# 64-slot experts: bank copies ahead of the next unit's rounding, the second projections eight units behind, one scatter a unit later

## The reference, cut to what matters

```
for e in range(N_EXPERTS):                                  # 8 experts, D_FF_EXPERT = 3584
    gate, up = split(x @ w_in[e])                           # 1024 x 7168
    out = out + gates[:, e:e+1] * ((silu(gate) * up) @ w_out[e])   # 3584 x 1024
```

## Time and profile before

| | us |
|---|---|
| median of 3 runs (lowest, highest) | 1513.35 (1511.95, 1513.36) |
| the profiled execution | 1512.7 |
| its span, first to last instruction | 1511.0 |
| the experts, PE's first unit to the end | 545.2 to 1511.0 |

### The profile page before, as it was taken

The page is one execution under the profiler, slowest core; times in us unless marked ns, Lnnn a source line. Parts: engine busy times, 40 slices in busy tenths (PEclk is TensorE's granted clock), DMA queues, the critical chain, the costliest instruction groups (busy, mean ns, idle before and its releaser), DMA issues.

```text
span 1511.0 us, 18519 instructions
## 1 busy us (share of the span) xinstructions
PE 1428.3 (95%) x7386; PEld 1210.5 (80%) x7386; DVE 1145.6 (76%) x791; ACT 959.0 (63%) x791; POOL 66.6 (4%) x69
## 2 busy tenths in 40 slices
PE   6999999999999899999989998899999889999996
PEld 6987779999899778877778886778887777888885
DVE  3456664444657578898998888899889899889886
ACT  4334544334444457768877777887777887777774
POOL 1001200000000142000001000001000000000000
PEclk9999999999999979999999999999999999999998
DMA  9554556555464459999999999999999999999990
GB/s 348 183 176 158 195 167 219 176 190 194 141 223 167 140 188 362 357 352 366 392 405 368 356 359 361 390 418 366 364 358 349 386 414 400 357 354 378 364 361 30
DMA packets 158695, 446.89 MB, mean 296 GB/s; under 512 B 7040, under 2 KB 45952, under 8 KB 158608
## 3 DMA queue, kind: packets, MB, share of 16 engines
q1 hardware_dynamic: 156784, 439.38, 79.7%
q0 software_dynamic: 1824, 6.33, 1.3%
HBM read 444.63 MB, written 1.05 MB: 295 GB/s over the span
## 4 chain that ended last, share of the span: by engine, by line
PE 78%; ACT 12%; DVE 9%; issue 1%; DMA 1%; DVEq 0%; POOL 0%; SPq 0%; ACTq 0%; POOLq 0%
PE ps L1396 22%; PE ps L1398 21%; PE ps L1397 21%; ACT whi L824 7%; PE ps L1836 3%; PE ps L1799 3%; PE ps L1800 2%; DVE wlo L945 2%; ACT whi_more L824 2%; DVE wlo_more L945 2%; PE ps L1716 1%; PE ps L1793 1%; DVE wlo L377 1%; DMA raw<-in_ret_w_in 1%; ACT up_rows L863 1%
## 5 line engine op out<-in xcount | busy, mean ns | idle before, releaser
L945 DVE TENSOR_TENSOR wlo<-raw,whi 128x2048 fp32r<-128x2048 f32 x209 | 475.0, 2290 | 66.6 <-ACT whi L824 65.8
L824 ACT ACTIVATE whi<-raw 128x2048 fp32r<-128x2048 f32 x208 | 395.9, 1915 | 125.5 <-PE ps L1398 99.1
L377 DVE TENSOR_TENSOR wlo<-raw,whi 128x2048 fp32r<-128x2048 f32 x81 | 185.8, 2294 | 160.9 <-ACT whi L370 160.9
L370 ACT ACTIVATE whi<-raw 128x2048 fp32r<-128x2048 f32 x83 | 158.7, 1912 | 156.5 <-PE ps L1398 151.4
L1396 PE MATMUL ps<-xT_hi,whi 128*128 128x256 f32 x576 | 164.2, 285 | 6.9 <-DVE wlo L377 6.9
L1396 PE MATMUL ps<-whi,xg_big 128*128 128x512 f32 x420 | 166.8, 397 | 0.0
L1398 PE MATMUL ps<-whi,xg_big 128*128 128x512 f32 x420 | 164.6, 392 | 0.0
L1397 PE MATMUL ps<-wlo,xg_big 128*128 128x512 f32 x420 | 164.4, 391 | 0.0
L1398 PE MATMUL ps<-xT_hi,wlo 128*128 128x256 f32 x576 | 163.8, 284 | 0.0
L1397 PE MATMUL ps<-xT_lo,whi 128*128 128x256 f32 x576 | 163.8, 284 | 0.0
L1396 PEld LDWEIGHTS ps<-xT_hi,whi 128*128 128x128 f32 x576 | 111.5, 193 | 7.7 <-issue 7.3
(11 more groups left out here) (251 smaller groups left out, 2761.7 us busy)
## 6 DMA issues: line engine op xcount, KB each, us to landing
raw<-in_moe_w_in SPq DMA_DIRECT2D x168, 1024.0 KB, 6.7
raw<-in_moe_w_out SPq DMA_DIRECT2D x84, 1024.0 KB, 7.0
more_raw<-in_moe_w_in SPq DMA_DIRECT2D x56, 1024.0 KB, 6.7
more_raw<-in_moe_w_out SPq DMA_DIRECT2D x28, 1024.0 KB, 6.8
raw<-in_ret_w_in SPq DMA_DIRECT2D x24, 1024.0 KB, 5.1
raw<-in_ffn_w_in SPq DMA_DIRECT2D x22, 1024.0 KB, 4.9
raw<-in_ffn_w_out SPq DMA_DIRECT2D x11, 1024.0 KB, 4.9
raw<-in_ret_w_out SPq DMA_DIRECT2D x8, 1024.0 KB, 4.8
```

Source lines behind the costliest of these rows:

```text
L370: nc.scalar.activation(whi[:, u % SPLIT, :], src, ACT.Copy).then_inc(hi_done, 1)
L377: nc.vector.tensor_tensor(wlo[:, u % SPLIT, :], src, whi[:, u % SPLIT, :].bitcast(F32), ALU.subtract).then_inc(lo_done, 1)
L824: nc.scalar.activation(moe_split(n)[0], moe_raw(n), ACT.Copy).then_inc(hi_done, 1)
L945: return nc.vector.tensor_tensor(dst, src, hi.bitcast(F32), ALU.subtract)
```

## The change

It has five parts, and adds or removes no instruction.
1. A small job has its own order of units. Between the last up unit of block 0 and its first out unit lie eight units instead of four (out 0 in units 16 to 19 instead of 12 to 15), and out 1, 2 and 3 come last, in units 32 to 41.
2. `gT_small` becomes two buffers, used in turn by the blocks.
3. ACT's copies of gate and up banks stand ahead of the rounding of the same step (`small_copies`), both gate banks in one step; the turns, Silu, product and low half move to later steps, and the rounding of the product leaves the step of the product (`SMALL_HI`).
4. The product on DVE waits for the low half of the block before it.
5. In all jobs scatter(0) stands behind unit 2 instead of unit 1, and DVE's first add in step 3 instead of step 2. scatter(1) stays behind unit 4 and the second add in step 5.

```diff
+    SMALL_STREAM = [(part, b, q) for part, b in (("gate", 0), ("up", 0), ("gate", 1), ("up", 1), ("out", 0), ("gate", 2),
+                                                 ("up", 2), ("gate", 3), ("up", 3), ("out", 1), ("out", 2), ("out", 3))
+                    for q in range(BLOCK_UNITS[b])]
...
-    SMALL_GATE = BIG_SILU
+    SMALL_GATE = {3: 0, 11: 1, 23: 2, 29: 3}
...
-        gT_small, _ = place("gT_small", [P, 8, P], F32R, at=gT_at)
+        gT_small = [place(f"gT_small{i}", [P, 8, P], F32R, at=gT_at + i * 4096)[0] for i in range(2)]
...
+            def small_copies(i, u):
+
+                if i in SMALL_GATE:
+                    unit_done(act, u + i, 0)
+                    for s in range(BLOCK_UNITS[SMALL_GATE[i]] // 2):
+                        nc.scalar.activation(gate_rows[:, s * BANK:(s + 1) * BANK], ps[:, s, :],
+                                             ACT.Copy).then_inc(gate_copied, 1)
+                if i in SMALL_UP:
+                    unit_done(act, u + i, 0)
+                    for s in range(BLOCK_UNITS[SMALL_UP[i]] // 2):
+                        nc.scalar.activation(up_rows[:, s * BANK:(s + 1) * BANK], ps[:, 2 + s, :],
+                                             ACT.Copy).then_inc(up_copied, 1)
...
                 for i in range(JOB_UNITS):
+                    if SMALL[j]:
+                        small_copies(i, u)
                     moe_hi(j * JOB_UNITS + i + MSPLIT)
...
+                    if 4 * small + b > 0:
+                        dve.wait_ge(small_lo, 4 * small + b)
...
-                        elif i in (2, 5):
-                            t, at = i // 3, 1 + POSITION[j - 1]
+                        elif i in (3, 5):
+                            t, at = i // 5, 1 + POSITION[j - 1]
...
-                    if j > 0 and i == 1:
+                    if j > 0 and i == 2:
                         pe.wait_ge(selT_ready, j)
                         pe.wait_ge(y_lo_done, 2 * j)
                         scatter(0)
```

More of the change, by code:

```diff
@@ L59, in build @@
     BLOCK_UNITS = [4, 4, 4, 2]
[L60 to L63, removed]
+    BIG_STREAM = [(part, b, q) for part, b in (("gate", 0), ("up", 0), ("gate", 1), ("out", 0), ("up", 1), ("gate", 2),
+                                               ("out", 1), ("up", 2), ("gate", 3), ("up", 3), ("out", 2), ("out", 3))
+                  for q in range(BLOCK_UNITS[b])]
+    SMALL_STREAM = [(part, b, q) for part, b in (("gate", 0), ("up", 0), ("gate", 1), ("up", 1), ("out", 0), ("gate", 2),
+                                                 ("up", 2), ("gate", 3), ("up", 3), ("out", 1), ("out", 2), ("out", 3))
+                    for q in range(BLOCK_UNITS[b])]
+    assert EFF == 3 * W + BANK and len(BIG_STREAM) == len(SMALL_STREAM) == JOB_UNITS and U_MOE % SPLIT == 0 and JOB_UNITS % RAW == 0
     HALF = P // 2
@@ L76, in build @@
     BIG_LO = {9: (0, 0), 11: (0, 1), 21: (1, 0), 23: (1, 1), 33: (2, 0), 35: (2, 1), 38: (3, 0)}
-    SMALL_GATE = BIG_SILU
[L78 to L82, removed]
+    SMALL_GATE = {3: 0, 11: 1, 23: 2, 29: 3}
+    SMALL_GATE_TURN = {5: 0, 12: 1, 24: 2, 32: 3}
+    SMALL_UP = {7: 0, 15: 1, 27: 2, 31: 3}
+    SMALL_UP_TURN = {8: 0, 16: 1, 28: 2, 33: 3}
+    SMALL_MUL = {9: 0, 17: 1, 29: 2, 34: 3}
+    SMALL_HI = {10: 0, 18: 1, 30: 2, 35: 3}
+    SMALL_LO = {12: 0, 20: 1, 32: 2, 37: 3}
     GATHER = {i: k for k, i in enumerate((13, 15, 17, 19, 25, 27, 29, 31))}
@@ L407, in again_landed, with moe_source @@
             eng.wait_ge(landed[i % RAW], 16 * (landings(i % RAW, MOE_UNITS) + i // RAW + 1) + 16 * (JOB_UNITS // RAW) * p)
-        def moe_source(i, e):
-            part, b, q = STREAM[i]
+        def moe_source(i, e, small=False):
+            part, b, q = (SMALL_STREAM if small else BIG_STREAM)[i]
             if part == "out":
@@ L479, in _, with moe_unit @@
                 load_unit(sp, U_ATT_OUT + i, 0, att_out[:, 2 * i:2 * i + 2, :], 2)
-            def moe_unit(u, i, e, slot, dst, free):
-                src, rows = moe_source(i, e)
+            def moe_unit(u, i, e, slot, dst, free, small=False):
+                src, rows = moe_source(i, e, small)
                 sp.wait_ge(lo_done, free)
@@ L500, in _ @@
                     back = MRAW if n >= MRAW else RAW
-                    moe_unit(U_MOE + n, i, e, moe_slot(n), moe_raw(n), U_MOE + n - back + 1 if n < RAW or n >= MRAW else U_MOE)
+                    moe_unit(U_MOE + n, i, e, moe_slot(n), moe_raw(n), U_MOE + n - back + 1 if n < RAW or n >= MRAW else U_MOE,
+                             SMALL[j])
             sp.wait_ge(over_ready, 1)
@@ L843, in big_drains @@
                     nc.scalar.activation(gT_hi[:, 4 * s:4 * s + 4, :], bank(6, 4), ACT.Copy).then_inc(big_hi, 1)
-            def small_drains(i, u, small):
[L847 to L851, removed]
+            def small_copies(i, u):
[9 more added lines that the diff above has]
+                                             ACT.Copy).then_inc(up_copied, 1)
+            def small_drains(i, u, small):
                 if i in SMALL_GATE_TURN:
@@ L858, in small_drains @@
                     nc.scalar.activation(act_small[:, 0:w], ps[:, 0, 0:w], ACT.Silu).then_inc(small_silu, 1)
[L859 to L866, removed]
+                if i in SMALL_HI:
+                    b = SMALL_HI[i]
                     c = 2 * BLOCK_UNITS[b]
@@ L869, in small_drains @@
                     act.wait_ge(small_mul, 4 * small + b + 1)
-                    nc.scalar.activation(gT_small[:, 0:c, 0:HALF],
+                    nc.scalar.activation(gT_small[b % 2][:, 0:c, 0:HALF],
                                          hid_small[:, 0:c * HALF].rearrange("p (c n) -> p c n", c=c),
@@ L1321, in small_drains @@
                     dve.wait_ge(small_hi, 4 * small + b + 1)
-                    lo_of(gT_small[:, 0:c, HALF:P], hid_small[:, 0:c * HALF].rearrange("p (c n) -> p c n", c=c),
-                          gT_small[:, 0:c, 0:HALF]).then_inc(small_lo, 1)
+                    lo_of(gT_small[b % 2][:, 0:c, HALF:P], hid_small[:, 0:c * HALF].rearrange("p (c n) -> p c n", c=c),
+                          gT_small[b % 2][:, 0:c, 0:HALF]).then_inc(small_lo, 1)
                 if i in SMALL_MUL:
@@ L1753, in big_unit @@
             def big_unit(i, u, big, job, x, hi, lo, before_gate, before_up):
-                part, b, q = STREAM[i]
+                part, b, q = BIG_STREAM[i]
                 if q == 0 and part == "gate":
@@ L1802, in small_unit @@
             def small_unit(i, u, small, job, hi, lo, before_gate, before_up):
-                part, b, q = STREAM[i]
+                part, b, q = SMALL_STREAM[i]
                 if q == 0 and part == "gate":
@@ L1824, in small_unit @@
                             w = slice((2 * c + half) * BANK, (2 * c + half + 1) * BANK)
-                            last = both(ps[:, 4 + half, :], gT_small[:, 2 * q + c, :], hi[:, w], lo[:, w],
+                            last = both(ps[:, 4 + half, :], gT_small[b % 2][:, 2 * q + c, :], hi[:, w], lo[:, w],
                                         b == 0 and q == 0 and c == 0, b == 3 and q == 1 and c == 1)
```

## The result

| | before | changed |
|---|---|---|
| median of 4 runs on the same chip (lowest, highest), us | 1513.36 (1511.95, 1513.66) | 1490.13 (1484.18, 1492.59) |
| the profiled execution, us | 1512.7 | 1488.92 |
| its span, us | 1511.0 | 1487.2 |

The ratio is 0.9843, 95% interval 0.9812 to 0.9873: faster by 1.6%. The forecast was 1489.5. So the close agreement of the first number is partly luck, and the size of the gain is 23 to 31 us.

What follows compares the result with a forecast made beforehand. PE bounds big jobs; in small jobs no engine is full and DVE waits for ACT's roundings. Terms 31.5 - 10.8 + 4.5 - 2.7 = 22.5, some 23 us with job 7, gave 1489.5 us; range 1481 to 1499.

Steps and rivals of the forecast that it cites:

- the ring of four: Small jobs: rounding i+4 needs PE's unit i; PE may run up to 2.6 us late before DVE goes idle.
- The new wait: PE before scatter(1), for DVE's first add, once in each small job: 3.1 us.
- the 0.43 of the entry: DVE's wait at each entry to a small job, from the big job's last round, said to stay: 0.43 us.
- The clock behind it: Small jobs: PE's lower clock level after the wait before scatter(1), likely in all three, 1.6 us each.
- The term of -10.8: Loss from the wait before scatter(1) in three small jobs: 3 x (2.0 delay + 1.6 lower clock) us.
- The start of the big jobs: Big jobs behind small ones: scatter(1) begins 1.5 us earlier against DVE's work, three times, +4.5 us.
- the 31.5: Gain in us from DVE's 32.8 us of waits in the small jobs going, all but some 1.3.
- More stretches at the lower clock: Small jobs: one more low-clock stretch each, 0.9 us on DVE, -2.7 us; bounds 0 and -13.
- The fourth rival: Small jobs: the clock falls again and again, eight stretches a job, 14 us slower, 1528 us; chance 0.05.
- its room: ACT in small jobs: copies ahead of roundings delay them, but the worked schedule has room to hide it.
- some 3 MB to spare: Transfers: 2.5 of 5.2 MB lying ready are drawn down in a small job, costing nothing.
- If ACT waits for DMA: Named sign that the forecast is wrong: ACT kept waiting for transfers; no size given.

Runs made afterwards that it cites:

- e5: The changed kernel with the bank copies behind the rounding of their step again: 1504.76 us, ratio 0.9942.
- e7: The kernel before with only the copies put ahead of the rounding, in its old steps and order of units: 1495.46 us, ratio 0.9887.
- e2: The changed kernel without part 5 (scatter(0) behind unit 1, first add in step 2): 1490.56 us, ratio 0.985.
- e1: The changed kernel with the first add back in step 2, scatter(0) still behind unit 2: 1475.79 us, ratio 0.9748.
- c0: The changed kernel run again with no edit, on another chip, as yardstick for e1, e2 and e4: 1482.71 us, ratio 0.9793.
- e4: The changed kernel with 13 matmuls that nobody reads ahead of scatter(1) in each small job, filling PE's wait: 1482.13 us, ratio 0.9792.
- e3: The changed kernel with the first add in step 2 and scatter(1) behind unit 5 instead of unit 4: 1480.54 us, ratio 0.9789.
- e6: The changed kernel with 12 of the 14 bank copies of a small job done twice on ACT: 1497.61 us, ratio 0.9885.
- e9: The changed kernel with transfers of the experts issued seven units ahead instead of eight: 1487.97 us, ratio 0.9837.

## Why the prediction was right, and where it was not

- **The bound and the mechanism** (DVE kept waiting through the ring of four by PE's waits): right. PE's waits for copies went, that for the product fell from 3.8 to 0.4 us (nothing above 0.3 was forecast), DVE's idle time went with them, small jobs of 101 to 104 were forecast and 100.4 to 103.3 came. DVE is 98.2 busy in them instead of the 100 named. That the copies' place matters is shown in both directions by e5 (21 us lost) and e7 (16.6 gained). The time of the experts alone, in one profile each, gives the order of the gains: 965.8 us before, 947.1 with the copies ahead (e7), 941.4 with the new order of units and the later steps too (e2), 935.8 to 937.6 with part 5 (the changed kernel), 930.0 with the first add back in step 2 (e1). The step from e7 to e2 goes over two chips and more than one edit; the later second projections were not run by themselves.
- **The new wait**, 3.1 us before scatter(1): right in place, waiter and releaser, 2.9 measured. Its cost with the clock up: 2.0 forecast, 2.2 less the 0.43 of the entry = 1.8 measured.
- **The clock behind it**: 1.6 us in all three small jobs was forecast. It falls in six of twelve, and costs 1.3 to 2.9 where it does. The term of -10.8 was, in the changed kernel's first profile, 2.2 + 5.0 + 3.7 us of DVE's idle time less the 1.3 of the entries = 9.6, and 3.5 + 2.2 + 2.2 - 1.3 = 6.6 in c0. That the idling brings the fall is supported by e4 (0 of 3 where it is filled) and by e3 (3 of 3 behind the moved wait), not proven. The kernel before has the same with its wait of 2.06: the level falls right behind it in jobs 1 and 5 and not in job 3. In job 5:

```profile
1146.43 0.47 PE L1742 MATMUL ps<-y_hi,selT 128*128 128x512 f32 x1 [2.06 <-DVE y_lo L945]
...
1147.10 0.63 PE L1742 MATMUL ps<-y_hi,selT 128*128 128x512 f32 x1
1147.52 0.63 PE L1743 MATMUL ps<-y_lo,selT 128*128 128x512 f32 x1
```

- **The start of the big jobs**, +4.5: right in size where it can be read, 1.5 us (10.6 to 9.1). But the sum books -10.8 and +4.5 under part 5, a loss of 6.3, and e2 shows that taking part 5 away costs 7.9 us instead of giving any back. Two things were missed. Without part 5 the small jobs are no shorter, since the wait before scatter(0) and its falls of the clock come back. And the big jobs get longer: I took the 0.74 before scatter(0) there for all that stood in that place, and it becomes 2.1 once PE enters them early. That the total came out all the same means that some of part 5's worth was booked in the 31.5, which takes all waits of DVE as gone; how much was not measured.
- **More stretches at the lower clock**, -2.7: wrong, none came. The idle time that was to bring them is not there either: 0.38 us for nearly every unit was forecast. In job 1, 42 units of 1.82, the turns (six of some 2.0 and two of 1.0) and the scatters (1.9) are 92 of the 100.4 us. Less the new wait of 2.9 that leaves 5.5, or 0.13 a unit: the 2.20 - 1.82 had left out the turns. The longest wait that is left is 0.8, and the clock stays at its upper level behind it in all twelve small jobs. The fourth rival has nothing for it. The rule on clocks that go up and down with very short idle times (the Trainium skill, "TensorE: Matmul & The Clock Gate", "A second HAM failure mode: psum-queue depth-cycling") is not borne out here for waits of 0.8 us and less; as PE waits so little, that is a weak test of it.
- **The sum**: 31.5 - 9.6 + 4.5 = 26.4 for the first profile, where the experts gained 28.2 (1.6 of it in jobs 0 and 7: 0.7 and 0.9); 31.5 - 6.6 + 4.5 = 29.4 for c0, with 1511.0 - 1481.0 = 30.0 gained. So the terms that missed are those of the clock: -10.8 was 6.6 to 9.6, and -2.7 was nothing. The forecast of 23 met the first median because the part ahead of the experts took 4.4 us more there.
- **ACT**: its room was said to be enough, and is, but e6 shows that it ends within the next 6 us.
- **Transfers**: "some 3 MB to spare" was wrong. I counted the lead against DVE's pace; ACT, which takes the units, is ahead of DVE by then (it rounds a unit at 999.0 that DVE takes at 1003.3) and meets the landing. "If ACT waits for DMA" was named as a sign of being wrong, and it does: 2.1 us over all the experts in the changed kernel's first profile, none before. DVE, with roundings in hand, does not wait behind it in jobs 3 and 5, and the gain stands. e9 shows the waits grow with one unit less of lead, to 17.2 us over all the experts:

```profile
ACT whi L829 <- DMA more_raw<-in_moe_w_in: 0.6, 1, 0.6
...
ACT whi L829 <- DMA raw<-in_moe_w_in: 0.3, 1, 0.3
```

  (job 5 of the changed kernel). The Trainium skill ("DMA: Bandwidth & Descriptors", "Where 436 GB/s comes from") puts the HBM side at about 358 GB/s for a core. Here, with one core at work, the measurements are above it: the small jobs of the changed kernel run at 386 to 398 GB/s and its big jobs 2, 4 and 6 at 387 to 389.

## What to carry to other kernels

Three engines pass buffers round a ring here. A wait of one engine costs something only beyond the ring's room, which was worked out as 2.6 us (an estimate from the durations, not measured by itself). So add up everything that makes the engine late in one round: the new wait together with the turn of 1.9 us behind it, not each alone. When one wait is taken away, look for every waiter of what was moved: the add here had two (scatter(1) and the transpose), and the best version by 7 us moved the scatter without moving the add. A part that is worth nothing alone (part 5, 0.9992) can be worth 8 us once the engine it serves is no longer late for other reasons.

## What the runs showed of the hardware that was not expected

Behind the same wait of 2.9 us, in the same program, PE's clock fell to the lower level in six small jobs of twelve and stayed up in six; over all profiles with that wait it fell in 16 of 24. Behind a wait of 2.06 it fell in two small jobs of three of the kernel before. With the wait filled with matmuls it fell in none of three. One fall costs the job 1.3 to 2.9 us: 1.3 to 1.6 where 5 or 7 matmuls run 0.43 us apart, 2.9 where it is 11.
